# Rows of a 64-row expert block spread over all 128 partitions for gathers, scatters and row tiles, in a two-layer MoE trunk on Trainium2

## The reference

```python
g = argmax(softmax(x @ w_group))                 # 1 group of 4 for each token
vals, idx = top_k(softmax((x @ w_expert)[group g]), 2)     # 2 experts of 8 in it
wts = max(gp) * vals / sum(vals)
for e in range(32):                              # rows that chose expert e
    hmid = silu(xb @ w_gate[e]) * (xb @ w_up[e])  # 1024 -> 512
    out  = hmid @ w_down[e]                       # 512 -> 1024
y[token] = sum over its 2 experts of wts * out
x = layer_norm(ALPHA * x + y, g, b)
```

## Time and profile before

| | us |
|---|---|
| median of 3 runs | 1573.11 (1571.71 to 1574.68) |
| the profiled execution | 1570.7 |
| its span, first to last instruction | 1568.9 |
| PE busy | 1329.2 (85%) |
| DVE busy | 409.9 (26%) |
| mean granted clock of PE | 0.948 |
| bytes moved by DMA | 472.70 MB, mean 301 GB/s |

### The profile page before, as it was taken

One profiled execution on the slowest core, in us unless ns is written; L12 is line 12 of the kernel. 1 busy time (PEld: TensorE's weight loads), 2 busy tenths in 40 slices (PEclk: granted clock), 3 DMA queues, 4 the chain that ended last, 5 costly groups with the idle time before them and its releaser, 6 DMA issues.

```text
span 1568.9 us, 19948 instructions
## 1 busy us (share of the span) xinstructions
PE 1329.2 (85%) x8334; PEld 907.0 (58%) x8334; DVE 409.9 (26%) x834; ACT 203.0 (13%) x325; POOL 190.6 (12%) x220
## 2 busy tenths in 40 slices
PE   7999998989987877778669999888998777787881
PEld 6888876656654444445348887665665444444440
DVE  1211113341111111111254764344111111111117
ACT  1000012010000000000044553111000000000011
POOL 0000000122221111111010000012221111111101
PEclk8999999799999999999969999989999999999995
DMA  9952204599999999999796112359999999999974
GB/s 228 321 218 107 79 31 155 198 385 411 396 417 408 414 407 418 414 407 422 258 283 265 55 54 110 120 222 391 404 399 408 405 416 405 414 413 400 421 270 107
DMA packets 94035, 472.70 MB, mean 301 GB/s; under 512 B 14256, under 2 KB 49072, under 8 KB 60171
## 3 DMA queue, kind: packets, MB, share of 16 engines
q1 hardware_dynamic: 79085, 447.35, 73.4%
q0 software_dynamic: 10048, 16.85, 3.1%
q10 hardware_dynamic: 4854, 7.84, 1.7%
HBM read 456.98 MB, written 23.06 MB: 306 GB/s over the span
## 4 chain that ended last, share of the span: by engine, by line
PE 47%; DMA 42%; DVE 6%; issue 2%; ACT 2%; POOL 1%; SPq 1%; POOLq 0%; ACTq 0%; DVEq 0%
PE ps L559 18%; DMA ring<-in_moe_w_up 17%; DMA ring<-in_moe_w_gate 16%; PE ps L797 11%; PE ps L643 7%; DMA ring<-in_moe_w_down 5%; PE ps L826 5%; DMA ring<-yrows 2%; PE ps L787 1%; DMA ring<-in_a_w_in 1%; PE ps L661 1%; DMA yrows<-A,Bt 1%; PE ps L695 1%; DVE C L1473 1%; DVE C L1532 1%
## 5 line engine op out<-in xcount | busy, mean ns | idle before, releaser
L797 PE MATMUL ps<-ring,A 128*64 128x256 f32 x4096 | 484.9, 393 | 104.2 <-DMA ring<-in_moe_w_up 72.0
L797 PEld LDWEIGHTS ps<-ring,A 128*64 128x64 f32 x4096 | 321.5, 142 | 284.5 <-issue 102.8
L559 PE MATMUL ps<-A,ring 128*128 128x260 f32 x1280 | 285.5, 385 | 2.9 <-DMA ring<-in_a_w_in 2.9
L826 PE MATMUL ps<-ring,C 128*64 128x512 f32 x1024 | 241.6, 614 | 40.6 <-DVE C L1461 14.3
L559 PEld LDWEIGHTS ps<-A,ring 128*128 128x128 f32 x1280 | 245.1, 192 | 41.2 <-issue 3.2
L1458 DVE TENSOR_TENSOR C<-C,ps 128x256 f32<-128x256 f32 x64 | 26.9, 421 | 727.1 <-ACT C L1077 727.1
L826 PEld LDWEIGHTS ps<-ring,C 128*64 128x64 f32 x1024 | 79.2, 140 | 159.4 <-issue 143.7
L498 POOL DMA_INDIRECT A<-x,idx x64 | 62.4, 975 | 458.1 <-PE ps L787 422.5
L643 PE MATMUL ps<-Bt,ring 128*128 128x260 f32 x512 | 116.1, 385 | 1.0 <-ACT C L998 0.8
L643 PEld LDWEIGHTS ps<-Bt,ring 128*128 128x128 f32 x512 | 96.1, 190 | 20.2 <-DVE A L1305 2.5
L1077 ACT ACTIVATE C<-ps 128x256 f32<-128x256 f32 x64 | 24.6, 384 | 527.0 <-PE ps L797 527.0
(11 more groups left out here) (215 smaller groups left out, 698.3 us busy)
## 6 DMA issues: line engine op xcount, KB each, us to landing
ring<-in_moe_w_gate SPq DMA_DIRECT2D x64, 2048.0 KB, 42.9
ring<-in_moe_w_up SPq DMA_DIRECT2D x64, 2048.0 KB, 42.4
ring<-in_moe_w_down SPq DMA_DIRECT2D x64, 2048.0 KB, 41.5
ring<-in_a_w_in SPq DMA_DIRECT2D x24, 512.0 KB, 7.4
ring<-yrows SPq DMA_DIRECT2D x10, 832.0 KB
ring<-in_b_w_in SPq DMA_DIRECT2D x8, 1024.0 KB, 12.0
yrows<-C SPq DMA_DIRECT2D x5, 832.0 KB
x<-C ACTq DMA_DIRECT2D x10, 416.0 KB
```

What stands on the lines that cost most here:

```text
L559: mm = pe.matmul(bank, lhs(k), rhs(k), start=(k == 0), stop=(k == KT - 1))
L797: mm = pe.matmul(ps[hf * ROWS:(hf + 1) * ROWS, 1, u * FH:(u + 1) * FH], xgT[:, k, :], ring[:, slot, col:col + FH], start=(k == 0), stop=(k ...
L826: mm = pe.matmul(ps[nh * ROWS:(nh + 1) * ROWS, 2, :], hidT[:, at:at + ROWS], ring[:, slot, m * D + nh * 512:m * D + (nh + 1) * 512], start ...
```

## The change

The block of an expert now has CAP = 64 places instead of 48, and a place's partition is chosen by the table `slotno`. Rank r stands in column 32*(r mod 2) + 4*((r div 2) mod 8) + (r div 16) of `rowhot`. The gather has 128 places: ranks with even number go to partitions 0 to 31, odd ones to partitions 64 to 95, and neighbours in rank stand 4 partitions apart; the other 64 places hold NOROW. For that PE computes `idx` with two matmuls per table, one for each half of PSUM's partitions. The turn has all 128 partitions (eight transposes of 128 x 128, over two PSUM banks instead of one), and DVE's multiplication picks the 64 used columns out of 128. `dest` has 128 places too, so one indirect DMA of 128 places scatters both halves. Gate and up move from PSUM bank 1 to bank 3, and `spread_norm` works in four pieces over banks 5, 6, 7, 5, with a wait for ACT before the fourth. The loads of the input tiles and the read of `yrows` take 128 rows instead of 104; the additional ones are not used.

```diff
-CAP = 48
+CAP = ROWS
+Q = ROWS // 2
 def rows_target(l, j, n):
-    return 32 * (l * len(range(j, END, UNROLL)) + n)
+    return 16 * (l * len(range(j, END, UNROLL)) + n)
...
-                    sp.dma_start(picks[l][i], rows_dram[i * TT:(i + 1) * TT]).then_inc(rows_in_sb[i], 16)
+                    sp.dma_start(pick_rows[l][i], rows_dram[i * TT:i * TT + P]).then_inc(rows_in_sb[i], 16)
...
-                sp.dma_start(xtok[:, i, :], a["x_prompt"][0, i * TT:(i + 1) * TT, :]).then_inc(x_in[i], 16)
+                sp.dma_start(xfull[:, i, :], a["x_prompt"][0, i * TT:i * TT + P, :]).then_inc(x_in[i], 16)
...
+            pool.iota(slotno[:, :], pattern=[[1, 2], [2, 8], [16, 4]], base=0, channel_multiplier=0,
+                      allow_small_or_imprecise_dtypes=True).then_inc(consts, 1)
+            pool.memset(idx[:, :], NOROW).then_inc(consts, 1)
...
                     pool.indirect_dma_start(
-                        out=xg[e % UNROLL][:CAP], out_offset=None, in_=x1_dram[l],
+                        out=xg[e % UNROLL], out_offset=None, in_=x1_dram[l],
...
                 def scatter(rows, where, done):
-                    for nh in range(2):
-                        pool.indirect_dma_start(
-                            out=half_rows, out_offset=bass.IndirectOffsetOnAxis(ap=where(nh), axis=0),
-                            in_=rows[nh * ROWS:nh * ROWS + CAP, :], in_offset=None,
+                    pool.indirect_dma_start(
+                        out=half_rows, out_offset=bass.IndirectOffsetOnAxis(ap=where, axis=0),
+                        in_=rows, in_offset=None, bounds_check=2 * TOPK * T - 1, oob_is_err=False,
...
                 for c in range(TOPK * NT):
-                    mm = pe.matmul(ps[:CAP, 5, :NE], rowhot[:, c, :], ohtok[:, c // NT, c % NT, :],
-                                   start=(c == 0), stop=(c == TOPK * NT - 1))
+                    for h in range(2):
+                        mm = pe.matmul(ps[h * ROWS:h * ROWS + Q, 5, :NE], rowhot[:, c, h * Q:(h + 1) * Q],
+                                       ohtok[:, c // NT, c % NT, :], start=(c == 0), stop=(c == TOPK * NT - 1))
...
-                        mm = pe.transpose(ps[:, 0, k * ROWS:(k + 1) * ROWS], xv[:, k, :], ident[:ROWS, :ROWS])
+                        mm = pe.transpose(ps[:, k // 4, (k % 4) * P:(k % 4 + 1) * P], xv[:, k, :], ident[:, :])
...
-                def spread_norm(g, b):
-                    for r, bank in ((g, (6, 7)), (b, (3, 5))):
+                def spread_norm(q, g, b):
+                    for n_, (r, h, bank) in enumerate(((g, 0, 5), (g, 1, 6), (b, 0, 7), (b, 1, 5))):
+                        if n_ == 3:
+                            pe.wait_ge(bc_ok, 4 * q + 1)
...
-                tt(rowhot, over10(v10(1), CAP), iota[:, :CAP].unsqueeze(1).broadcast_to([TT, TOPK * NT, CAP]),
+                tt(rowhot, over10(v10(1), ROWS), slotno[:, :].unsqueeze(1).broadcast_to([TT, TOPK * NT, ROWS]),
                    ALU.is_equal).then_inc(hot_ok, 1)
...
-                tsc(idx[:, :NE], ps[:CAP, 5, :NE], float(NOROW), ALU.add).then_inc(idx_ok[l], 1)
+                for h in range(2):
+                    b = slice(h * ROWS, h * ROWS + Q)
+                    ins = tsc(idx[b, :NE], ps[b, 5, :NE], float(NOROW), ALU.add)
+                ins.then_inc(idx_ok[l], 1)
...
-                    tt(xgT, ps[:, 0, :KT * ROWS].rearrange("p (k t) -> p k t", k=KT),
-                       gb[:, 2 * l, :].unsqueeze(2).broadcast_to([P, KT, ROWS]), ALU.mult).then_inc(half, 1)
+                    turned = ps[:, 0:2, :].rearrange("p b (k h u q) -> p (b k) h u q", h=2, u=2, q=Q)
+                    tt(xgT.rearrange("p k (h q) -> p k h q", h=2), turned[:, :, :, 0, :],
+                       gb[:, 2 * l, :].unsqueeze(2).unsqueeze(3).broadcast_to([P, KT, 2, Q]), ALU.mult).then_inc(half, 1)
```

More of the change, by code:

```diff
@@ L44 @@
 NOROW = 4096
+CONSTS = 17
 NODEST = 8192
@@ L135, in build @@
         ones = sb("ones", [TT, TT], BF16)
-        iota = sb("iota", [TT, max(CAP, NBLK)])
+        iota = sb("iota", [TT, NBLK])
+        slotno = sb("slotno", [TT, ROWS], BF16)
         thr = sb("thr", [TT, MAXQ])
@@ L166, in build @@
         gain, shift = Bt[:TT, 0:D], Bt[:TT, D:2 * D]
-        picks = [[ring[:TT, ring_slot(POS_EXP[l] + 3 * (END - 1) + i // 2), (i % 2) * 2 * D:(i % 2 + 1) * 2 * D]
-                  .rearrange("t (k d) -> t k d", k=TOPK) for i in range(NT)] for l in range(DEPTH)]
+        pick_rows = [[ring[:, ring_slot(POS_EXP[l] + 3 * (END - 1) + i // 2), (i % 2) * 2 * D:(i % 2 + 1) * 2 * D]
+                      .rearrange("t (k d) -> t k d", k=TOPK) for i in range(NT)] for l in range(DEPTH)]
+        picks = [[r[:TT] for r in rows] for rows in pick_rows]
         zeros = C[:TT, 5 * D + 256:5 * D + 768]
@@ L212, in build @@
         picked = sb("picked", [TT, NT, NE], BF16)
-        dest = Bt[:CAP, rt[0]:rt[0] + 2 * NBLK].bitcast(I32).rearrange("p (h b) -> p h b", h=2)
-        assert rt[0] + 2 * NBLK <= 7 * 512, rt[0]
-        xg = [A[:ROWS, i * D:(i + 1) * D] for i in range(UNROLL)]
+        dest = Bt[:, rt[0]:rt[0] + NBLK].bitcast(I32)
+        assert rt[0] + NBLK <= 7 * 512, rt[0]
+        xg = [A[:, i * D:(i + 1) * D] for i in range(UNROLL)]
         xgT = A[:, 3 * D:3 * D + KT * ROWS].rearrange("p (k t) -> p k t", k=KT)
@@ L520, in _ @@
                         pool.wait_ge(y_act[l], d + 1)
-                        scatter(yo[d % UNROLL], lambda nh: dest[:, nh, d:d + 1], y_out[d % UNROLL])
+                        scatter(yo[d % UNROLL], dest[:, d:d + 1], y_out[d % UNROLL])
                 n_over = pool.value_load(over_i[0:1, OVER:OVER + 1], min_val=0, max_val=OVER)
@@ L1022, in norm_rows @@
                 def norm_rows(q, scale):
-                    for v, (out, bank) in enumerate(((gain, (6, 7)), (shift, (3, 5)))):
-                        act.wait_ge(bc_mm, 2 * q + v + 1)
-                        for h in range(2):
-                            ins = act.activation(out[:, h * 512:(h + 1) * 512], ps[:TT, bank[h], :], ACT.Copy, scale=scale)
-                    ins.then_inc(bc_ok, 1)
+                    for n_, (out, h, bank) in enumerate(((gain, 0, 5), (gain, 1, 6), (shift, 0, 7), (shift, 1, 5))):
+                        act.wait_ge(bc_mm, 4 * q + n_ + 1)
+                        act.activation(out[:, h * 512:(h + 1) * 512], ps[:TT, bank, :], ACT.Copy,
+                                       scale=scale).then_inc(bc_ok, 1)
                 def square(m):
@@ L1163, in _ @@
             tt, stt = dve.tensor_tensor, dve.scalar_tensor_tensor
+            for nh in range(2):
+                dve.memset(dest_base[nh * ROWS:(nh + 1) * ROWS, :], float(NODEST + nh)).then_inc(consts, 1)
             for n_, i in enumerate(FIRST_ORDER):
@@ L1440, in overflow @@
                     dve.wait_ge(idx_mm, 3 * l + 3)
-                    tsc(idx[:, NE:], ps[:CAP, 5, 128:128 + OVER], float(NOROW), ALU.add)
-                    for nh in range(2):
-                        tsc(dest[:, nh, :NE], ps[:CAP, 5, 64:64 + NE], float(NODEST + nh), ALU.add)
-                        tsc(dest[:, nh, NE:], ps[:CAP, 5, 192:192 + OVER], float(NODEST + nh), ALU.add)
+                    for h in range(2):
+                        b = slice(h * ROWS, h * ROWS + Q)
+                        tsc(idx[b, NE:], ps[b, 5, 128:128 + OVER], float(NOROW), ALU.add)
+                    tsc(dest[:, :NE], ps[:, 5, 64:64 + NE], dest_base[:, 0:1], ALU.add)
+                    tsc(dest[:, NE:], ps[:, 5, 192:192 + OVER], dest_base[:, 0:1], ALU.add)
                     dve.tensor_copy(over_i[:, OVER:], cum[0:1, NE - 1:])
```

100 lines of the change are left out of this document (51 added, 49 removed).

## The result

The changed kernel takes 1517.39 us (median of 4 runs, 1516.27 to 1521.73) beside 1572.41 for the kernel before (4 runs, 1570.3 to 1574.68). The ratio is 0.9655, 95% interval 0.9631 to 0.9679: 3.45% faster, 55 us. The profiled execution took 1517.84 with a span of 1516.0, so the span is 52.9 us shorter than before.

The account below looks back on a forecast made before the run. DMA engines set the pace for 26.3 experts a layer, slowed by writes not filling 128 partitions. -2 + 2 x (4.4 - 5.0 - 19.2 - 4.5 + 2.5) = -45.6 from 1570.7 gives 1525, predicted median 1527; range 1512 to 1567.

Parts of the forecast that it names:

- Gathers, -19.2 a layer: Expert loops: the 0.73 us an expert lost behind each gather goes wholly, for 26.3 experts a layer; bounds -19.2 and 0.
- balance, -4.5: Expert loops: rows dealt more evenly over 16 engines regain half of 0.34 us an expert; -4.5 us a layer, bounds -8.9 and 0.
- skipped places, +2.5: Expert loops: 112 more skipped places an expert in the indirect DMAs, at 11 ns each, cost +2.5 us a layer.
- the slow stretch: Expert loops: three us after each gather at 321 instead of 430 GB/s, 0.76 us once an expert.
- Routing, +4.4 a layer: Before expert 0: doubled matmul sums for idx, overflow and dest +4.0, wider rowhot +0.2, one more DVE instruction +0.2.
- Layer end, -5.0: End of each layer: one scatter less to issue, -0.9, and faster yrows tiles of 128 rows, -4.1 us.
- Start, -2: Program start, once: input tiles of 128 rows load at 430 instead of 237 GB/s; -2 us, bounds -3 and +1.6.
- the slow stretch stays: Expert loops: rates still fall behind gathers, from reading scattered DRAM rows or the indirect DMA as such; 1566 us, chance 0.18.
- places are dealt in runs of eight: Gathers and scatters: runs of eight consecutive partitions put the gather's rows on eight engines; slower, 1587 us, chance 0.12.
- DRAM limits the wide reads: Input and yrows tiles: reads stay at 190 GB/s with 23% more bytes; 1542 us, chance 0.10.
- the rule that the prediction cites: DMA: in a transfer to 128 partitions each engine writes one SBUF port, partitions 4e to 4e+3 and 32 above, likewise upper half.
- above 415: Expert loops, sign of being right: windows of the DMA rate stay above 415 GB/s after a gather.

Follow-up runs that it names:

- the two kernels with 64 places: Changed kernel with gathers cut from 128 places to 64: into partitions 32 to 95, 1521.76 us; into partitions 0 to 63, 1570.08 us.
- the snake: Changed kernel with only the table slotno edited, ranks from 32 on dealt in the opposite direction: 1514.83 us, ratio 0.9634.
- the kernel with partitions 32 to 95: Changed kernel with gathers of 64 places instead of 128, written to partitions 32 to 95: 1521.76 us, ratio 0.9674.
- narrow tiles: Changed kernel with the loads of the input tiles and the reads of yrows back at 104 rows: 1528.34 us, ratio 0.9712.
- the plain order: Changed kernel with only the table slotno edited, rank r in column r of rowhot: 1532.46 us, ratio 0.9749.
- an empty 128: Changed kernel with one more gather behind each scatter, of 128 places that all hold NOROW: 1524.06 us, ratio 0.9685.

## Why the prediction was right

1527 was predicted and 1517.39 measured, within the range. The gains that it summed were all seen, and one cost, that of the routing, was not. The sizes, by step:

- *Gathers, -19.2 a layer, and balance, -4.5, against skipped places, +2.5.* Together -21.2. The loops gained 20.5 and 19.0 us from expert 0 to the last scatter. In layer 0 some 1.7 of it are PE's clock: it was granted 0.81 on average from 284 to 293 us before (0.54 in the first 3 us, 1.00 in the last 3) and 1.00 from 280 to 289 after, and expert 0's product took 8.81 and 7.13 us. So about 19 was right, 2 less than the sum. I took the whole of the slow stretch to go; that it was the destination's partitions is shown by the two kernels with 64 places, not only argued. The skipped places cost some 9 ns and not 11: 112 x 9 / 16 x 26.3 = 1.7 a layer. The balance improved in part, as assumed, but the half was never measured by itself: in layer 0 the run-down shrank from 14 us at a mean share of 0.62 to 8 us, and the snake removed most of the rest.
- *Routing, +4.4 a layer: the term that was mis-sized.* The step that failed is "Records so short are nearer to being limited by their number, so +4.0". The sums for `idx` doubled their matmuls and became shorter, 1.81 to 1.28 us, and those for `dest` took 3.33 instead of 2.82, not 3.3 and 5.3. The two halves do overlap, the bound "+0" that I had named and not taken, and a record got cheaper with its width, from 48 columns to 32. The kernels with 64 places show both: their 10 matmuls of 64 columns for `idx`, 20 records, took 2.34 us where 20 of 48 columns had taken 1.81, in proportion to the width. At that price 40 records of 32 columns one behind the other would take about 2.4 us (an estimate from these two), and they took 1.28. All three stretches ran at a granted clock of 0.50, the lower level. In the chain of the kernel with partitions 32 to 95:

```profile
271.13 2.34 PE ps L773 x20
```

  The sums for both tables together cost nothing more a layer and not 4.0, so the term was too high by 8.0 us in the two layers.
- *Layer end, -5.0.* -4.5 in layer 0, where DVE's wait for the second tile went as predicted. Layer 1 gained 3.4: there PE's `add_end`, done later than the tiles, was next, which I had reckoned only for layer 0.
- *Start, -2.* -2.8 at the mixer. The rate was near the 430 GB/s assumed: the window of 4 to 7 us reads 412 here and 249 with narrow tiles. The sum's own figures give 3.1 us, of which it took only 2.
- *What I did not see:* 3.0 us at the very end. The page counts no DRAIN as busy, and the chain ended with DVE; I never asked what lay between DVE's last instruction and the span's end, 7.8 us before and 4.8 after.

In the profiled executions the sum missed 7.3 us (45.6 for 52.9): too little by 8.0 in the routing's sums, 3.0 in the DRAIN, 1.7 in the clock and 0.8 at the start, too much by 3.6 in the loops, 2.1 at the ends and 1.0 between the layers. That adds up to 6.8; 0.5 stay open. So errors of 13.5 us one way were offset by 6.7 the other way, and it is partly luck that the forecast lies no further off. The rest of the 10 us is that the median lay 2.4 above the profiled execution before and 0.5 below it after.

The rival that the slow stretch stays is refuted by the windows; that places are dealt in runs of eight, by the result itself and by the price of the plain order, 15.1 us where the counts by engine gave 18; that DRAM limits the wide reads, by 426 GB/s. The rate behind a gather, 401 to 414, was a little under the "above 415" that I had asked for.

## What to carry to other kernels

Look for stretches in which the rate of all transfers falls behind one small copy that fills fewer than 128 partitions, and pad or move it: 128 places, or 64 in partitions 32 to 95, kept the full rate here; 48 in 0 to 47 and 64 in 0 to 63 did not. Then count rows by engine and not by transfer, since a ring waits for the slowest engine. And ask what each engine still has to do behind its last useful instruction: a drain moved into idle time gave 4.2 us with 64 places.

## What the hardware showed that I had not expected

- A gather of 64 places into partitions 0 to 63, of which by the rule that the prediction cites only half are written by an engine that is not theirs, slowed the transfers as far as the 48 places before did: 324 against 321 GB/s.
- POOL's final DRAIN depends on the kernel's indirect DMAs and repeats to 0.01 us: 9.49 (gathers of 48, two scatters of 48), 6.48 (128 and 128, in four kernels), 10.96 (64 and 128, in three), 9.50 (128, 128 and an empty 128). It does not grow with the number of DMAs (126 in both the second and the third form, 188 in the others) nor with that of places, and what sets it is open. The narrow tiles left it at 6.48.
- Forty matmul records of 32 columns, alternating between the two halves of PSUM's partitions, took 1.28 us; twenty of 64 columns with the same sums took 2.34, twenty of 48 took 1.81, all at a granted clock of 0.50.
